# All expert loads issued by the sync engine in one line, in the order in which their buffers come free

## The reference, cut to what matters

```python
def moe(h, router_w, router_b, wg, wu, wd, swg, swu, swd):
    ...                                     # sigmoid scores, 4 of 8 groups, top 8 of 64 experts
    routed = routed_experts(x, eidx, w, wg, wu, wd)
    shared = (jax.nn.silu(x @ swg) * (x @ swu)) @ swd
    return (routed + shared).reshape(B, S, D)

# in routed_experts, for the tokens xb of one expert e:
    hb = jax.nn.silu(xb @ wg[e]) * (xb @ wu[e])
    return (hb @ wd[e]) * w[:, None]
```

## Time and profile before

| what | value |
|---|---|
| median of 3 runs | 1442.52 us (1441.85 to 1442.69) |
| the profiled execution, its own time | 1440.6 us |
| its span from first to last instruction | 1438.8 us |
| mean granted TensorE clock | 0.997 |
| TensorE busy | 1397.9 us, 97% of the span |
| moved by DMA | 509.52 MB, mean 354 GB/s |
| queue q1 (SP) | 370.42 MB |
| queue q10 (ACT) | 119.54 MB |
| 28 passes of layer 0 | about 247 to 707 us |
| 28 passes of layer 1 | about 956 to 1418 us |

### The profile page before, as it was taken

The page is one execution under the profiler, slowest core; times in us unless marked ns, Lnnn a source line. Parts: engine busy times, 40 slices in busy tenths (PEclk is TensorE's granted clock), DMA queues, the critical chain, the costliest instruction groups (busy, mean ns, idle before and its releaser), DMA issues.

```text
span 1438.8 us, 20775 instructions
## 1 busy us (share of the span) xinstructions
PE 1397.9 (97%) x8288; PEld 707.9 (49%) x8288; DVE 437.5 (30%) x1161; ACT 317.1 (22%) x746; POOL 48.1 (3%) x86
## 2 busy tenths in 40 slices
PE   7999999999999999999999999999999999999997
PEld 3345656444444444544465456564444445444433
DVE  1146435312221222221345143442122212132114
ACT  2134323111111111111345122411111111111113
POOL 0100301000000000000100010010000000000000
PEclk9999999999999999999999999999999999999999
DMA  9999528999999999999972246289999999999992
GB/s 392 386 383 427 218 94 321 391 402 427 411 424 427 419 426 426 423 427 425 406 298 118 117 161 239 91 361 404 405 427 417 425 420 422 425 425 424 426 419 88
DMA packets 48003, 509.52 MB, mean 354 GB/s; under 512 B 5809, under 2 KB 6209, under 8 KB 8321
## 3 DMA queue, kind: packets, MB, share of 16 engines
q1 hardware_dynamic: 27728, 370.42, 61.9%
q10 hardware_dynamic: 16416, 119.54, 20.1%
q0 software_dynamic: 3760, 18.20, 3.4%
HBM read 499.10 MB, written 11.01 MB: 355 GB/s over the span
## 4 chain that ended last, share of the span: by engine, by line
PE 87%; DMA 5%; DVE 3%; ACT 3%; issue 1%; ACTq 0%; SPq 0%; DVEq 0%
PE bank L2029 25%; PE banks L2079 13%; PE banks L1931 10%; PE banks L442 5%; DMA s_dn_ring<-in_moe_wd_dram 4%; PE ybank L1959 3%; PE banks L1119 3%; PE banks L1959 3%; PE bank L1961 3%; PE bank L504 2%; PE ybank L1723 1%; PE banks L1723 1%; DMA s_gu_ring<-in_ada_w_dram 1%; PE banks L697 1%; PE banks L1124 1%; PE banks L671 1%
## 5 line engine op out<-in xcount | busy, mean ns | idle before, releaser
L2029 PE MATMUL bank<-s_gu_ring,s_hbuf 128*32 128x512 f32 (+1 forms) x2688 | 395.3, 593 | 0.9 <-DVE s_hbuf L2160 0.9
L2029 PEld LDWEIGHTS bank<-s_gu_ring,s_hbuf 128*32 128x32 f32 (+1 forms) x2688 | 122.2, 119 | 264.7 <-issue 264.7
L2079 PE MATMUL banks<-s_dn_ring,s_hTs 128*32 128x512 f32 (+1 forms) x1344 | 205.9, 602 | 4.9 <-DMA s_dn_ring<-in_moe_wd_dram 4.9
L2205 DVE TENSOR_TENSOR s_ylo<-banks,s_yhi 128x512 fp32r<-128x512 f32 x112 | 77.5, 692 | 327.0 <-ACT s_yhi L2121 327.0
L1931 PE MATMUL banks<-s_sel,s_htok 128*128 128x512 f32 (+1 forms) x640 | 144.8, 374 | 0.5 <-issue 0.5
L1931 PEld LDWEIGHTS banks<-s_sel,s_htok 128*128 128x128 f32 x640 | 106.3, 188 | 60.7 <-issue 44.3
L2121 ACT CAST s_yhi<-banks 128x512 fp32r<-128x512 f32 x112 | 65.7, 586 | 303.3 <-PE banks L2079 303.3
L2079 PEld LDWEIGHTS banks<-s_dn_ring,s_hTs 128*32 128x32 f32 (+1 forms) x1344 | 56.8, 119 | 123.9 <-issue 123.2
L2200 DVE SCALAR_TENSOR_TENSOR s_hh<-s_sg,s_wsl,bank 128x256 f32<-128x256 f32 x56 | 26.9, 480 | 287.2 <-ACT s_sg L2112 287.2
L2112 ACT ACTIVATE s_sg<-bank 128x256 f32<-128x256 f32 x56 | 21.6, 385 | 364.0 <-PE bank L2029 364.0
L2160 DVE COPY s_hbuf<-banks 128x512 f32<-128x512 f32 (+1 forms) x60 | 39.4, 656 | 96.0 <-PE banks L1931 96.0
(11 more groups left out here) (463 smaller groups left out, 1452.9 us busy)
## 6 DMA issues: line engine op xcount, KB each, us to landing
s_gu_ring<-in_moe_up_dram SPq DMA_DIRECT2D x128, 2048.0 KB, 16.2
s_dn_ring<-in_moe_wd_dram ACTq DMA_DIRECT2D x114, 1024.0 KB, 17.0
s_gu_ring<-in_ada_w_dram SPq DMA_DIRECT2D x24, 2048.0 KB, 14.3
s_dn_ring<-in_moe_wd_dram SPq DMA_DIRECT2D x14, 1024.0 KB, 11.2
s_gu_ring<-in_win_dram SPq DMA_DIRECT2D x6, 2048.0 KB, 12.0
s_gu_ring<-in_wqkv_dram SPq DMA_DIRECT2D x6, 1024.0 KB, 19.5
s_gu_ring<-in_wo_dram SPq DMA_DIRECT2D x2, 2048.0 KB, 20.5
s_gu_ring<-in_shared_up_dram SPq DMA_DIRECT2D x2, 2048.0 KB, 10.7
```

Source lines behind the costliest of these rows:

```text
L2029: last = pe.matmul(W0[o:o + n, :], tokens_of(p, k)[:, o:o + n], w[:, k, :, :], start=(k == 0), stop=(k == KC - 1))
L2079: last = pe.matmul((W1, W2)[half][o:o + n, :], hTs[:, f, o:o + n], dn_ring[:, DN_PLACE[dn_of[(l, r)][0]], w0:w0 + 512], start=(f == 0), st ...
L2205: dve.tensor_tensor(ylo[:, half, :], (W1, W2)[half], yhi[:, half, :].bitcast(F32), ALU.subtract).then_inc(S["y_low"], 1)
```

## The change

All expert loads are issued by SP. Its program, after the loads at fixed ranks and those of the ring's start, walks over the passes: for each pass it issues as many up loads as the pass has experts (each waits for gu_full of that pass), and then the down loads, in the order of LOAD_ORDER, whose slots are free by y_full of that pass. A new table, down_free, says for each load after which pass its slot is free. A down load is never issued before one that stands ahead of it in LOAD_ORDER, so load 9 now follows load 8, at pass 2. ACT's issues are taken out.

```diff
-        gu_of, dn_of = {}, {}
+        gu_of, dn_of, down_free = {}, {}, {}
...
+            freed = [None] * (NDN - 1) + [2]
             for r in LOAD_ORDER[l]:
...
+                down_free[(l, r)], freed[d] = freed[d], pass_of[l][r]
...
                 sp.wait_ge(S["order_full"], l + 1)
-                for i, r in enumerate(LOAD_ORDER[l]):
-                    if i < NFIX:
-                        continue
+
+                def load_up(r):
+
                     e = sp.value_load(order[0:1, r:r + 1], min_val=0, max_val=NE - 1)
                     s, _, used = gu_of[(l, r)]
                     if used:
                         sp.wait_ge(*used)
                     sp.dma_start(gu_ring[:, s, :], w_up[e]).then_inc(slot_in[s].h, 16)
-                    if i < DN_EARLY:
-                        d = dn_of[(l, r)][0]
-                        sp.dma_start(dn_ring[:, DN_PLACE[d], :], wd[e].rearrange("(p f) n -> p (f n)", p=P)).then_inc(down_in[d].h, 16)
-
-                for r, _ in PASSES[l][NP - 1]:
+
+                def load_down(r):
+
                     e = sp.value_load(order[0:1, r:r + 1], min_val=0, max_val=NE - 1)
                     d, _, used = dn_of[(l, r)]
-                    sp.wait_ge(*used)
+                    if used:
+                        sp.wait_ge(*used)
                     sp.dma_start(dn_ring[:, DN_PLACE[d], :], wd[e].rearrange("(p f) n -> p (f n)", p=P)).then_inc(down_in[d].h, 16)
 
+                for i in range(NFIX, NGU):
+                    load_up(LOAD_ORDER[l][i])
+                    if i < DN_EARLY:
+                        load_down(LOAD_ORDER[l][i])
+                up, down = NGU, DN_EARLY
+                for p in range(NP):
+                    for r, _ in PASSES[l][p]:
+                        if up < NE:
+                            load_up(LOAD_ORDER[l][up])
+                            up += 1
+                    while down < NE and down_free[(l, LOAD_ORDER[l][down])] <= p:
+                        load_down(LOAD_ORDER[l][down])
+                        down += 1
...
                             act.copy(yhi[:, half, :], (W1, W2)[half]).then_inc(S["y_high"], 1)
-                        for r in LOAD_ORDER[l][DN_EARLY:len(LOAD_ORDER[l]) - len(PASSES[l][NP - 1])]:
-                            d, _, used = dn_of[(l, r)]
-                            if used == (S["y_full"], 2 * (l * NP + p + 1)) or (p == 2 and used == (S["shd_used"], l + 1)):
-                                e = act.value_load(order[0:1, r:r + 1], min_val=0, max_val=NE - 1)
-                                act.wait_ge(*used)
-                                act.dma_start(dn_ring[:, DN_PLACE[d], :], a["moe_wd"][l][e].rearrange("(p f) n -> p (f n)", p=P)).then_inc(down_in[d].h, 16)
```

## The result

| | kernel before | changed kernel |
|---|---|---|
| median of the runs | 1442.24 us (1440.63 to 1445.68, 6 runs) | 1435.12 us (1434.76 to 1436.99, 6 runs) |
| ratio | | 0.9950 (95% interval 0.9937 to 0.9962) |
| profiled execution, own time / span | 1440.6 / 1438.8 us | 1434.92 / 1433.1 us |
| mean granted clock of it | 0.997 | 0.997 |

The change makes the kernel 0.5% faster, 7.1 us; 4.6 to 5.0 were forecast (1437.5). On the chip of the later runs on load 8, one execution of the kernel before took 2120.91 us and one of the changed kernel 8019.40; both stand far outside all others and are left out of every median, range and ratio of those two kernels.

A forecast was written before the change was run, and what follows sets the result against it. TensorE (97% busy) and, over long stretches, the DMA engines were both taken as full. Gains of 2.0 and 2.6 us made 4.6 off 1442.5, 1437.9, or 1436.2 with a second clock lowering; 1437.5 was taken, range 1435.0 to 1441.3.

The forecast's parts named there:

- The wait moves and shrinks: Pass 26's dn_ring waits (2.49, 2.58 us) become gu_ring waits at pass 27 of 0.5 and 1.65 us; chance 0.60.
- The wait vanishes whole: Rival: down loads leave sooner, one line loses less between transfers, no wait remains; gain 6.8 to 8.5 us, chance 0.10.
- No change: Rival: service order is not issue order (1442.5), or the lower clock follows the new wait (1439.6); chance 0.25.
- Slower: Rival: 2.47 us of hole lost in both layers, lower clock after both new waits, 1446.3 us; chance 0.05.
- The hole early in the layer: Near 310 us, load 9 behind load 8 takes 2.47 us of work from the queue; bounds 0 to 2.47, taken 0.
- 0.7 us sooner issue: Down loads leave SP some 0.7 us sooner, not behind ACT's copies; worth 0 with full DMA engines, but for the hole.
- The sum: Over both layers, waits removed minus new waits: 2.0 us in layer 0, 2.6 in layer 1, together 4.6 us.
- The second lowering of the clock: After layer 0's wait, a possible 1.70 us loss explaining the timed runs' extra 1.9 us; removing it gives 1436.2 us.
- something constant: Whole kernel: the timed runs' extra 1.9 us over the profiled execution stays, giving 1437.9 us.

The follow-up runs named there:

- the tail swapped: Changed kernel with down loads 59 and 60 issued a pass later, behind up loads 62 and 63: 1447.46 us, ratio 1.0037.

## Why the prediction was right, and where it was off

**The wait moves and shrinks: right.** Order is shown as the main cause from both sides: two loads put ahead give 0.997, the same two put behind give 1.004. Load by load in layer 0: down 59 and 60 landed at 679.4 and 681.9 (forecast 679.1, 681.5), up 62 and 63 at 686.8 and 691.6 (686.5, 691.4), and the new wait was 0.56 us (0.5). The last three down loads came 2.9 us early (3). In the earlier trace rows a load issued 5 us later arrived 4 us sooner; with all 256 expert loads in one queue, every one of them landed in the order of issue. The Trainium skill ("DMA: Bandwidth & Descriptors", section "Queues, rings and completion order") says that an engine with work in several queues serves them in turn, a packet at a time. The traces agree on the turns: load 62 overtook load 60 by 4.3 us in two queues and no load overtook another in one; the size of a packet is shown by no run here.

**The rivals.** "The wait vanishes whole" did not hold: gu_ring waits remain. "No change" did not hold. The Trainium skill (same page, section "Issuing engines are not separate DMA queues") says that issuing from several engines saves issue time only. The order of arrival did change here (down load 60 landed at 681.9, ahead of up load 62 at 686.8, and behind it before), so the rule can't be read as "the order is the same". "Slower" did not come, but the hole it was built on is real.

**The hole early in the layer: priced right by luck.** I let load 8 leave at the end of pass 2, 308.0. Its slot is freed by the shared expert's down matmuls, inside that pass, and SP issued it at 301.4; ACT had issued it at 308.5 only because its program stood behind the copies of pass 2. I said that an issue at 308 would leave no hole; held there, it cost some 3 us. And I said that each us of hole makes load 63 later by a us. The changed kernel does have a hole, at 288 to 296 and not near 310: 278 GB/s against 407 before are 1.03 MB, 2.4 us at 424 GB/s. Up load 63 of layer 0 landed no later for it, 444.2 after the first gate-up matmul in both kernels, because the kernel before fell short in its turn right after:

```profile
288.00:296.00 8.00, 8.00 (x64) 3.50 (x56) 0.72 (x2) 0.97 (x2) 0.00 (x0) 1.00 1.02 407
...
304.00:312.00 8.00, 8.00 (x77) 2.46 (x80) 1.96 (x5) 1.17 (x2) 0.00 (x0) 1.00 0.95 381
312.00:320.00 8.00, 8.00 (x52) 4.84 (x44) 1.17 (x2) 1.34 (x3) 0.00 (x0) 1.00 0.98 388
```

These two windows are 1.5 us short of 424 GB/s, the rest of the lead went by 387 us: over the 140 us from the first gate-up matmul both kernels moved the same, 407 GB/s. The term came out as 0 since load 8 left 7 us sooner than I thought and since the kernel before had no lead left to lose. "0.7 us sooner issue" was right for the down loads in general and wrong by a factor of ten for load 8.

**The sum: three terms off in size.** In the span 5.7 us were gained (1438.8 to 1433.1) where I had 4.6. Layer 0 gave 1.9 (2.0 forecast). Layer 1 gave 3.9 (2.6), since up load 63 landed at 1398.5 and not at 1399.6, and its wait was 0.35 and not 1.65 us. Passes began 0.2 us later. Counted from the layer's first gate-up matmul, its landing in layer 1 was 445.3 and 445.0 in the two profiles of the kernel before, 444.0 in both of the changed kernel, and from 443.6 to 445.5 in the two profiles with only two loads moved. One landing scatters by 1 to 2 us from one profile to the next, as much as the term that I built on it (1.65); why the changed kernel's come sooner is not settled.

**The second lowering of the clock: the alternative that I weighed too low.** Between my profiled run and the median lay 1.9 us; I leaned to "something constant". The profile of the kernel before, taken again, shows two lowerings. The waits themselves fell by 2.49 + 2.58 - 0.56 - 0.35 = 4.2 us. The fastest runs of the two kernels, on different chips, are 1438.84 and 1434.76 us, 4.1 apart; the medians are 7.1 apart. The runs of the kernel before spread over 3 to 7 us on the several chips, with mean clocks of 0.998 to 0.994, those of the changed kernel over 2.2 us with 0.998 to 0.996. So about 4 us of the gain are the waits themselves and about 3 us the clock. This split is argued from the runs' mean clocks and from the profiles (the kernel before: one and two lowerings; the changed kernel: none and one); no experiment changed the clock alone, and one lowering in each kernel's second profile lies in the mixer, where the change does nothing. Against the forecast: 4.6, + 1.3 for layer 1's landing, - 0.2 for the start, + 1.4 (the medians lie 1.6 us above the profiled run before and 0.2 after, which fits a second lowering that the median run of before had and its profiled run had not), is 7.1.

## What to carry to other kernels

With two queues before DMA engines that were full, a load's time of issue said little about its landing (5 us later, 4 us sooner). In such a kernel, list landings against needs, find the one load that is late, and ask what was moved ahead of it that is needed later. When a load waits for a buffer, look for the event that frees it and for what else stands ahead of the issue in its engine's program; a release inside a stage can be 7 us before the stage's end. Profile the kernel before twice before pricing a term of 1 us.

## What the runs showed of the hardware

- **A short wait can cost more than itself, and its length does not tell.** After a TensorE wait of some 2.5 us the clock fell to half for 3.4 us, 1.7 us lost, in some executions and not in others: after layer 1's wait but not layer 0's in one, the reverse in the other. The latter shows a lowering in layer 1's mixer too, at 878 us, where no expert load was waited for; one of the changed kernel's profiles has it near 875 us. The profile with load 8 held back waited 3.40 us in layer 0 and kept its upper level (granted 1.00 over 690 to 698), while a wait of 4.05 us with the tail swapped was followed by 6.8 us of lowered clock, part of it during the wait.
- **One landing scatters by 1 to 2 us** between executions of the same kernel, after 440 us of a queue that is all but full: 443.6 and 445.5 in layer 1 with two loads moved, 443.9 and 445.3 in layer 0 with load 9 first.
- **A lead in a full pipeline is lost, a lag is not made up.** 2.2 us of bytes gained at 297 us were gone by 387 us, and 7.4 us of work left out in layer 1 brought the last up load in only 3.2 us sooner; 1 us of hole at 308 us was still there at 690 us. A hole is free where it only uses up such a lead.
- **In one queue the loads landed in the order of issue,** all 256 of them, 1 and 2 MiB mixed; in two queues an up load overtook a down load issued 5 us before it.
